# Hyena convolution jobs of two chunks queued alternately, with two sets of tree buffers, batched products and paired sums

## The reference, cut to what matters

```
z = v
for o, gate in enumerate((x1, x2)):
    zf = jnp.fft.rfft(z, n=2 * L, axis=1)
    conv = jnp.fft.irfft(zf * resp[None, :, o], n=2 * L, axis=1)[:, :L]
    z = gate * (conv + z * bias[o])
```

## Time and profile before

| | us |
|---|---|
| median of 3 runs | 4882.63 (4880.24 to 4887.17) |
| the profiled execution | 4888.32 |
| its span, first to last instruction | 4886.5 |
| share of the span busy: PE, DVE, ACT, POOL | 86%, 51%, 21%, 25% |
| convolutions, first tree step to last gate's end | 3227.25 to 3742.74 |

### The profile page before, as it was taken

One profiled execution on the slowest core, in us unless ns is written; L12 is line 12 of the kernel. 1 busy time (PEld: TensorE's weight loads), 2 busy tenths in 40 slices (PEclk: granted clock), 3 DMA queues, 4 the chain that ended last, 5 costly groups with the idle time before them and its releaser, 6 DMA issues.

```text
span 4886.5 us, 50801 instructions
## 1 busy us (share of the span) xinstructions
PE 4181.5 (86%) x21784; PEld 3487.2 (71%) x21784; DVE 2472.8 (51%) x2798; ACT 1028.2 (21%) x1392; POOL 1201.7 (25%) x674
## 2 busy tenths in 40 slices
PE   6799888888679999999678988966664799999998
PEld 3488777777468888888557777755554678888886
DVE  1465155555235444444465554548885264444443
ACT  1233212112122111111223233211111221111112
POOL 1221233333143222222410000012222332222224
PEclk8799699999789999999888888888887999999999
DMA  9511000000201111111122122132221101111111
GB/s 352 191 45 43 21 1 1 1 1 1 95 26 35 35 39 36 39 39 38 60 67 66 63 73 89 52 132 79 80 80 63 32 28 39 36 39 39 36 40 61
DMA packets 253817, 280.43 MB, mean 57 GB/s; under 512 B 7942, under 2 KB 217815, under 8 KB 249080
## 3 DMA queue, kind: packets, MB, share of 16 engines
q1 hardware_dynamic: 253592, 277.18, 17.0%
HBM read 219.48 MB, written 57.67 MB: 57 GB/s over the span
## 4 chain that ended last, share of the span: by engine, by line
PE 72%; DVE 17%; DMA 3%; issue 3%; ACT 2%; POOL 2%; SPq 1%; POOLq 0%; DVEq 0%; ACTq 0%
PE PS L590 52%; DVE piece L1465 8%; PE PS L1533 7%; DVE piece L1019 3%; PE PS L990 2%; PE PS L991 2%; DVE piece L516 2%; DMA piece<-in_l_ada_w 2%; PE PS L1703 2%; PE PS L986 2%; PE PS L702 1%; DVE piece L509 1%; DVE piece L1406 1%; SPq L338 0%; ACT piece L1754 0%
## 5 line engine op out<-in xcount | busy, mean ns | idle before, releaser
L590 PE MATMUL PS<-piece,piece 128*128 128x512 f32 (+1 forms) x13824 | 2754.2, 361 | 162.3 <-POOL piece L534 97.5
L590 PEld LDWEIGHTS PS<-piece,piece 128*128 128x128 f32 x13824 | 2312.3, 191 | 607.1 <-issue 153.5
L573 POOL TENSOR_TENSOR piece<-piece,piece 128x1024 fp32r<-128x1024 f32 (+1 forms) x204 | 499.6, 2450 | 2468.0 <-ACT piece L567 2468.0
L1533 PE MATMUL PS<-piece,piece 128*128 128x256 f32 x1920 | 436.1, 388 | 138.6 <-DVE piece L1465 90.6
L1406 DVE SCALAR_TENSOR_TENSOR piece<-piece,piece,piece 128x1024 f32<-128x1024 f32 x352 | 534.9, 1520 | 12.6
L1533 PEld LDWEIGHTS PS<-piece,piece 128*128 128x128 f32 x1920 | 371.3, 195 | 200.7 <-issue 128.3
L1426 DVE SCALAR_TENSOR_TENSOR piece<-PS,piece,piece 128x1024 f32<-128x1024 f32 x224 | 187.8, 880 | 415.4 <-PE PS L590 415.4
L567 ACT ACTIVATE piece<-piece 128x1024 fp32r<-128x1024 f32 (+1 forms) x204 | 205.0, 1007 | 678.2 <-PE PS L590 636.0
L1019 DVE TENSOR_TENSOR piece<-piece,PS 128x512 f32<-128x512 f32 x288 | 185.4, 684 | 254.0 <-PE PS L991 196.7
L1403 DVE TENSOR_SCALAR piece<-piece,piece 128x1024 f32<-128x1024 f32 x44 | 35.8, 813 | 483.5 <-ACT piece L1367 483.5
L1465 DVE TENSOR_TENSOR piece<-piece 128x512 f32<-128x512 f32 (+2 forms) x168 | 163.2, 971 | 87.5 <-ACT piece L1953 68.2
(11 more groups left out here) (209 smaller groups left out, 3888.9 us busy)
## 6 DMA issues: line engine op xcount, KB each, us to landing
piece<-in_l_ada_w SPq DMA_DIRECT2D x24, 2048.0 KB, 18.1
piece<-in_l_ffn_up SPq DMA_DIRECT2D x88, 512.0 KB, 3.7
piece<-in_l_w_in SPq DMA_DIRECT2D x44, 512.0 KB, 5.5
piece<-in_l_ffn_down SPq DMA_DIRECT2D x48, 384.0 KB, 3.0
filters_s<-piece SPq DMA_DIRECT2D x8, 2176.0 KB, 6.6
piece<-filters_s SPq DMA_DIRECT2D x8, 2176.0 KB, 8.1
hyena_tokens<-piece SPq DMA_DIRECT2D x24, 640.0 KB, 4.5
piece<-hyena_tokens SPq DMA_DIRECT2D x12, 1280.0 KB, 5.4
```

The costliest lines, as they stand in the source:

```text
L573: eng.tensor_tensor(LO[i % 2][0][:, 0:n], RAW[i % 2][:, 0:n], HI[i % 2][1][:, 0:n], ALU.subtract)\
L590: m = eng.matmul(PS[:, bank + b, 0:n], w, x[:, a:a + n], start=first and n_ == 0, stop=last and n_ == 2)
L1533: m = eng.matmul(PS[:, bank, o * HC:(o + 1) * HC], M[i][o], rhs[i], start=i == 0, stop=i == 1)
```

## The change

The two orders of two chunks are queued alternately: (chunk 0, order 0), (1, 0), (0, 1), (1, 1), then the same of chunks 2 and 3. Job k uses the set k % 2 of K, T and Z; the second set of K and T lies in those halves of HH and HL that chunks 2 and 3 fill. The tree of job k+1 stands in VectorE's list between the products of job k and its untree. The products take a leaf's both halves at once against a repeated filter row, and the s leaves 2 to 7 two at a time; GpSimd's sums take two leaves at a time. X1 and X2 become one buffer X, loaded for the next job after the gates (or, where X holds a result, after its turn). The turn of an order-1 job runs during the job behind it, or at the end; its low half is taken by VectorE straight from PSUM. XT is reloaded during the last job, and TensorE waits for IV only ahead of the first inverse.

```diff
+            set_a = [x_r.take(16, HC), x_r.take(16, HC), x_r.take(4, HC), x_r.take(4, HC)]
+            k_r, t_r = Region(HT_AT + KD // 2 * N, HT_AT + KD * N), Region(HT_AT + KD * N + KD // 2 * N, FIX_AT)
+            set_b = [k_r.take(16, HC), t_r.take(16, HC), k_r.take(4, HC), t_r.take(4, HC)]
...
+            Z, X = [mid.take(NT, HC) for _ in range(2)], mid.take(NT, HC)
+            QUEUE = [(c + i, order) for c in range(0, NCH, 2) for order in range(2) for i in range(2)]
+            XB = [X] * (nj - 1) + [Z[0]]
+            turns = [k for k, (c, order) in enumerate(QUEUE) if order]
...
+            BATCH = {"s": ((0, 1), (1, 1), (2, 2), (4, 2), (6, 2)), "p": ((0, 1), (1, 1))}
...
             # SP, for job k
+                    if k + 1 < nj:
+                        for g in "ps":
+                            eng.wait_ge(veC[g].sem, veC[g].at(taken(g, last_leaf(g)), k))
+                            eng.dma_start(HB[g], filt_dram[g][JOBS.index(QUEUE[k + 1])]).then_inc(s_h[g], 16)
...
+                    if k + 1 == nj - 1:
...
+                        for g in "ps":
+                            eng.wait_ge(veU[g].sem, veU[g].at("gate", k))
+                        eng.dma_start(XT, spill).then_inc(s_x, 16)
+                    elif k + 1 < nj:
+                        if order:
+                            eng.wait_ge(peO.sem, peO.at("t1", c))
+                        else:
+                            for g in "ps":
+                                eng.wait_ge(veU[g].sem, veU[g].at("gate", k))
+                        eng.dma_start(X, tok_dram[1 + QUEUE[k + 1][1], QUEUE[k + 1][0]]).then_inc(s_xg, 16)
...
             # TensorE, for job k
                     for l in LEAVES["s"]:
                         if l == N_BANKS["s"]:
+                            if k == 0:
+                                eng.wait_ge(s_iv, 16)
                             for lp in LEAVES["p"]:
+                                inverse("p", lp, k)
+                        if k - 2 in turns and l in (0, 3):
+                            eng.wait_ge(veO.sem, veO.at(f"lo{l // 3}", QUEUE[k - 2][0]))
+                        forward("s", l, k, [T[:, 2 * l, :], T[:, 2 * l + 1, :]])
                     for l in LEAVES["s"]:
+                        inverse("s", l, k)
+                    if k - 1 in turns and k < nj - 1:
+                        eng.wait_ge(acC["s"].sem, acC["s"].at(f"i{last_leaf('s')}", k))
+                        turn(k - 1)
...
             # GpSimd
+                        for a in LEAVES[g][::2]:
+                            kr, ki, tr, ti = quarters(K, T, a)
+                            eng.wait_ge(veC[g].sem, veC[g].at(taken(g, a + 1), rnd))
+                            eng.tensor_tensor(kr, kr, ti, ALU.subtract).then_inc(*smC[g].did(f"re{a}", rnd))
+                            eng.tensor_tensor(ki, ki, tr, ALU.add).then_inc(*smC[g].did(f"im{a}", rnd))
...
             # VectorE: multiply
+                    for l, n in BATCH[g]:
+                        both = PS[:, bank:bank + n, :].rearrange("p n (u c) -> p n u c", u=2)
...
+                        eng.wait_ge(peZ[g].sem, peZ[g].at(f"z{l + n - 1}", rnd))
+                        eng.tensor_tensor(keep, both, near, ALU.mult).then_inc(*ve.did(f"near{l}", rnd))
+                        eng.tensor_tensor(other, both, cross, ALU.mult).then_inc(*ve.did(f"cross{l}", rnd))
+                def spread(k):
+                    for half in range(2):
+                        eng.wait_ge(acO.sem, acO.at(f"hi{half}", c))
+                        eng.tensor_tensor(HL[:, 2 * c + half, :], psum(3 * half, N), HH32[:, 2 * c + half, :], ALU.subtract).then_inc(*veO.did(f"lo{half}", c))
...
+                start(0)
+                for k in range(nj):
+                    multiply("p", k)
+                    multiply("s", k)
+                    if k + 1 < nj:
+                        start(k + 1)
+                    if k - 1 in turns and k < nj - 1:
+                        spread(k - 1)
...
+                    gate("p", k, "it0", 4.0)
+                    untree(eng, veU["s"], "it", k, K, T)
+                    gate("s", k, f"it{N_INV - 1}", 1.0)
+                spread(nj - 2)
+                spread(nj - 1)
```

More of the change, by code:

```diff
@@ L1854, in mixer_hyena @@
-                poC[g] = steps("po_conv_" + g, [f"{t}{l}" for l in L for t in ("a", "b")], nj)
-            peO, acO, poO = steps("pe_turn", ["t0", "t1"], NCH), steps("ac_turn", ["hi0", "all0", "hi1", "all1"], NCH), steps("po_turn", ["lo0", "lo1"], NCH)
+                veC[g] = steps("ve_product_" + g, [f"{t}{l}" for l, n in BATCH[g] for t in ("near", "cross")], nj)
+                smC[g] = steps("po_sum_" + g, [f"{t}{a}" for a in L[::2] for t in ("re", "im")], nj)
+                veU[g] = steps("ve_unfold_" + g, [f"it{i}" for i in range(N_INV if g == "s" else 1)] + ["gate"], nj)
@@ new lines, in turn @@
+                def turn(k):
+                    c = QUEUE[k][0]
+                    for g in "ps":
+                        eng.wait_ge(veU[g].sem, veU[g].at("gate", k))
+                    for half in range(2):
+                        if k == turns[-1]:
+                            eng.wait_ge(veO.sem, veO.at(f"lo{half}", c - 1))
+                        for tt in range(NT):
+                            m = eng.transpose(PS[:, 3 * half + tt // 4, (tt % 4) * P:(tt % 4 + 1) * P], XB[k][:, tt, half * P:(half + 1) * P], ident)
+                        m.then_inc(*peO.did(f"t{half}", c))
@@ L1922, in _ @@
+                for k, (c, order) in enumerate(QUEUE):
+                    eng.wait_ge(s_z[k % 2], 16 * (c // 2 + 1))
                     if order:
-                        eng.wait_ge(veC["p"].sem, veC["p"].at("gate", rnd - 1))
+                        eng.wait_ge(veU["p"].sem, veU["p"].at("gate", k - 2))
                     for l in LEAVES["p"]:
-                        wait_conv_bank(eng, "p", rnd, "z", l)
-                        forward("p", l, [Z[:, NS // P + u, :] for u in range(2)])
@@ L1946, in _ @@
+                eng.wait_ge(acC["s"].sem, acC["s"].end())
+                for g in "ps":
+                    eng.wait_ge(veU[g].sem, veU[g].end())
+                turn(nj - 2)
+                turn(nj - 1)
             @program("ac")
@@ L1948, in _ @@
                 ended(eng, *part1)
-                for rnd, (c, order) in enumerate(JOBS):
+                def spread(k):
+                    c = QUEUE[k][0]
+                    for half in range(2):
+                        eng.wait_ge(peO.sem, peO.at(f"t{half}", c))
+                        eng.activation(HH[:, 2 * c + half, :], psum(3 * half, N), ACT.Copy).then_inc(*acO.did(f"hi{half}", c))
+                for k, (c, order) in enumerate(QUEUE):
                     for g in "ps":
                         for l in LEAVES[g]:
[L1952 to L1962, removed]
@@ L1967, in _ @@
                     for g in "ps":
[L1968 to L1971, removed]
-                            eng.tensor_tensor(K[:, 2 * l + 1, :], K[:, 2 * l + 1, :], T[:, 2 * l + 1, :], ALU.add).then_inc(*poC[g].did(f"b{l}", rnd))
@@ L1973, in _ @@
[L1973 to L1976 removed]
+                        K, T = KB2[rnd % 2][g], TB2[rnd % 2][g]
+                        for a in LEAVES[g][::2]:
[3 more added lines that the diff above has]
+                            eng.tensor_tensor(ki, ki, tr, ALU.add).then_inc(*smC[g].did(f"im{a}", rnd))
@@ L2019, in mixer_hyena @@
-            done = [peO, acO, poO] + [x[g] for x in (peC, acC, veC, poC) for g in "sp"]
+                        both = PS[:, bank:bank + n, :].rearrange("p n (u c) -> p n u c", u=2)
+                        keep, other = (b[:, 2 * l:2 * (l + n), :].rearrange("p (n u) c -> p n u c", u=2) for b in (K, T))
+                        if l == 0:
+                            near = ends(H, 2 * len(LEAVES[g]))
+                        else:
+                            near = H[:, 2 * l:2 * (l + n), :].rearrange("p (n u) c -> p n u c", u=2)[:, :, 0:1, :].to_broadcast([P, n, 2, HC])
@@ new lines, in start, with gate @@
+                def start(k):
+                    c, order = QUEUE[k]
+                    eng.wait_ge(s_z[k % 2], 16 * (c // 2 + 1))
+                    if k >= 2:
+                        for g in "ps":
+                            eng.wait_ge(veU[g].sem, veU[g].at("gate", k - 2))
+                    tree(eng, veT, "zt", k, Z[k % 2], 0, Z[k % 2], 0, KB2[k % 2]["s"], TB2[k % 2]["s"])
+                def gate(g, k, last, scale):
+                    order = QUEUE[k][1]
+                    dst = XB[k] if order else Z[k % 2]
+                    eng.wait_ge(veU[g].sem, veU[g].at(last, k))
+                    eng.wait_ge(*((s_xg, 16 * (k + 1)) if k < nj - 1 else (s_xl, 16)))
+                    f, n = FIRST[g], T_OF[g]
+                    eng.scalar_tensor_tensor(row(dst, f, n), row(TB2[k % 2][g], 0, n), scale, row(XB[k], f, n), ALU.mult, ALU.mult).then_inc(*veU[g].did("gate", k))
@@ L2020, in mixer_hyena @@
```

(3 more changed lines are left out.)

162 lines of the change are left out of this document (64 added, 98 removed).

## The result

The changed kernel takes 4831.66 us (median of 4, 4830.18 to 4835.59) where the kernel before took 4884.18 (4880.24 to 4887.17): a ratio of 0.9894, 95% interval 0.9877 to 0.9911, so 52 us faster. Forecast were 45 us and 4838.

The account below looks back on a forecast made before the run. Bound: a serial chain, mostly VectorE's, with one 8 us hole. Seven jobs of 57.2, a last of 50.7 and low halves 6.0 gain 43.4, with the weights 45.0: 4838 us, own range 4820 to 4856, chance 0.70.

Parts of the forecast that it names:

- The hole: In each job VectorE waits 8.14 us for TensorE's last eviction before the untree; the next job's tree was to fill it.
- The products: VectorE's filter products from PSUM: 683 ns for 512 columns, about 1.22 us for 1024, 11.6 us a job.
- the rival of contending products: VectorE's products also lose time beside GpSimd's sums: 5.3 us a job, 42 in all, so 4880; chance 0.06.
- The new wait: VectorE's last product batch, s leaves 6 and 7, waits 4.8 us a job for TensorE's leaf 7; products end at 16.5.
- TensorE's lost clock: After its pause TensorE runs at 1.2 GHz for about 3.8 us as the p inverses begin, losing 1.9 us.
- The rival in which it keeps its clock: TensorE still at 2.4 GHz when the p sums arrive: 1.9 us a job saved, 15 in all, 4823; chance 0.10.
- the one in which it never regains it: TensorE stays at 1.2 GHz because its matmuls come in shorter bursts: slower, about 4926; chance 0.06.
- The tree: The next job's tree behind the products: 14.94 us alone, plus 2.5 lost beside GpSimd's last sums, 17.4 in all.
- That the tree keeps GpSimd out: VectorE's tree wins each time, delaying GpSimd's last pair of sums: 4.4 us in seven jobs, 31, so 4869; chance 0.08.
- Jobs: Length of one job from its first product: 57.2 us against a mean of 64.1; 60 with low halves, 51 the last.
- Transfers: DMA loads: p gate's wait for X at most 1.0 us in two jobs, taken as 0; filters hidden; XT's reload gains 1.6.
- Behind the last gate: Turns, evictions and low halves after the last gate: taken as equal to the 12.2 us of before, plus or minus 3.

## Why the prediction was right, point by point

*The hole.* Right, and shown from both sides: in the plain jobs the 8 us are gone with the tree in them, and a hole of up to 9.8 comes back when it is taken out.

*The products.* Priced at 0.683 and 1.22, measured as follows in the groups of the changed kernel:

```profile
L2036 DVE TENSOR_TENSOR piece<-PS,piece 128x1024 f32<-128x1024 f32 x24 | 29.2, 1218 | 40.9 <-PE PS L1538 40.9
...
L2036 DVE TENSOR_TENSOR piece<-PS,piece 128x512 f32<-128x512 f32 x32 | 21.8, 681 | 0.0
```

They cost no more beside GpSimd's sums, so the rival of contending products is out. The Trainium skill (SBUF — State Buffer, "Who interferes with whom"; SBUF is the core's on-chip memory) says that a VectorE instruction with at most one SBUF input, outside its two-port modes, does not contend with GpSimd. The trace agrees: 681 ns here, 683 in the earlier trace rows.

*The new wait.* Forecast as 4.8 a job, measured as 40.9 / 8 = 5.1. The product phase was to be 16.5 and is 16.1 to 17.6. TensorE's lost clock was put at 1.9; the two p inverses and s leaves 6 and 7, 7.0 at full clock, took 8.6 to 10.1 until the batch, so 1.6 to 3.1 went, 2.3 in the mean. The rival in which it keeps its clock is out, and so is the one in which it never regains it.

*The tree.* Forecast 17.4, measured 16.84 (3363.99 to 3380.83): the two sums took 1.9 from it, not 2.5. The engines took turns, and the sums stretched as well. This 0.6 in seven jobs is 4 us, and the untree's 21.7 instead of 21.9 in eight is 1.5. Against them stands TensorE's clock: the product phase lasted 16.8 in the mean, some 2 us more in all. So the stage came out at 467.9 where the forecast's sum has 472.0 (3227.25 to 3699.3); misses of both signs make up these 4 us. That the tree keeps GpSimd out was a rival at 4869: not so, the sums ended within 4.6 us of its start.

*Jobs.* Plain ones 57.2 forecast; 56.2, 57.4, 56.1, 57.3 and 56.0 measured. With low halves 60.2; 59.8 and 59.1. The last 50.7; 51.1.

*Transfers.* X was put at 0 and at most 1.0, twice. It was 0 and 0.2:

```profile
3500.48 0.69 DVE L2058 SCALAR_TENSOR_TENSOR piece<-piece,piece 128x512 f32<-128x512 f32 x1 [0.20 <-DMA piece<-hyena_tokens]
```

That margin is thin: take the batch's wait away, and the p gate waits 1.9 for X. The filters were hidden, as said. IV's wait is named in the prediction, without a price. Its paragraph on the jobs compares with a mean of 64.1 that leaves out the first job's 69.6, but its sum is taken from the stage's two ends, so the 8 us are in the 45 all the same.

*Behind the last gate.* Equal chains were forecast: 12.2 before, and 11.3 now (3687.14 to 3698.41). The reload was put at 1.6: the tile was used 5.48 us after its issue before and 4.19 now, 1.3 less, and with the 1.0 of the chain this is the 2.3 between the two kernels. In the experiment that moves the reload alone it is worth 2.6.

*The sum.* 45.0 was forecast, 49.9 measured in stage and tail. Of the 52 by medians the other 2 are within what executions differ by ahead of the stage. In the forecast's range, minus 20 stands for seven trees without their 2.5, which is 17.5, and 4820 to 4856 has no room beside the tree's loss for the 3 of the tail. The measured time lies inside it.

## What to carry to other kernels

When a chain of engines leaves the busiest one a hole in each step, put the next step's independent work there, and then look at once for the next wait: here it was a batch that waited for its last leaf, worth 25 us and removed by one reordering. Look at the first step too: a wait that stands in it alone was worth 8 us here. A wider instruction saves time on its own engine (11.6 us of products a job instead of 13.25) and delays everybody who needed its first half; alone it made this kernel slower. Each wait removed used up the slack of another (the turn, then X), so price the slack of every cover that a faster path will meet.

## What the runs showed of the hardware

The time for which TensorE stayed at 1.2 GHz after a pause differed between neighbouring jobs of the same program. Windows of the changed kernel from the moment the p inverses begin, columns as above:

```profile
3295.50:3301.50 6.00, 5.95 (x14) 4.82 (x15) 4.25 (x4) 0.60 (x1) 6.00 (x6) 0.50 0.21 84
3352.90:3355.90 3.00, 2.91 (x7) 2.40 (x8) 3.00 (x3) 0.00 (x0) 3.00 (x3) 0.50 0.43 180
```

After pauses of 19.73 us in both, the clock was half for the first 6.0 us in one job and for 3.0 in the next (0.89 in the microsecond behind); those two jobs are the 57.4 and the 56.1 above. And where VectorE's tree steps and GpSimd's sums ran side by side without a pause, neither was shut out: in four steps and two sums VectorE lost 1.9 us (5.83 against 3.94) and the sums 1.9 (4.43 against 2.52).
